# The first DeltaNet step of each layer: roundings, masks, one block load and the places of the level products

## What is computed

```python
SEQ, D_MODEL, DEPTH = 1024, 1024, 2
DN_HEADS, DN_DK, DN_DV, DN_CHUNK = 8, 128, 128, 64
qkv = silu(causal_conv(concat([dq, dk, dv]), conv_w))
...
def gated_deltanet(q, k, v, beta, g):
    gc = cumsum(g)                                   # inside a chunk
    decay = exp(where(causal, gc[:, None] - gc[None, :], -inf))
    L = where(strict, (k * beta) @ k.T * decay, 0)   # strictly lower triangle
    sol = triangular_solve(L + eye, concat([v * beta, k * beta * exp(gc)]))
    u, w = split(sol)
    attn = (q @ k.T) * decay
    # then over the chunks, in order:
    v_new = u - w @ state
    o = (q * exp(gc)) @ state + attn @ v_new
    state = state * exp(gc_last) + (k * exp(gc_last - gc)).T @ v_new
```

## Time and profile before

| | |
|---|---|
| median of 3 runs | 2674.55 us |
| the profiled execution's own time | 2673.82 us |
| its span, first to last instruction | 2672.0 us |
| TensorE busy | 2637.4 us (99%) |
| VectorE busy | 1728.2 us (65%) |
| ScalarE busy | 679.5 us (25%) |
| GpSimd busy | 827.1 us (31%) |
| DMA engines, mean busy share of slices | 1 to 5 tenths |

### The profile page before, as it was taken

The page is one execution under the profiler, slowest core; times in us unless marked ns, Lnnn a source line. Parts: engine busy times, 40 slices in busy tenths (PEclk is TensorE's granted clock), DMA queues, the critical chain, the costliest instruction groups (busy, mean ns, idle before and its releaser), DMA issues.

```text
span 2672.0 us, 39928 instructions
## 1 busy us (share of the span) xinstructions
PE 2637.4 (99%) x14850; PEld 2254.4 (84%) x14850; DVE 1728.2 (65%) x3856; ACT 679.5 (25%) x1367; POOL 827.1 (31%) x455
## 2 busy tenths in 40 slices
PE   7999999999999999999999999999999999999998
PEld 5788888888888899888878888888888998888886
DVE  7878777877756555434587778777877555653333
ACT  5333333232312222200142332323232211230001
POOL 3233323333312122435422333332323122133443
PEclk9999999999999999999999999999999999999999
DMA  4322222222211112434532222222222111133344
GB/s 171 96 79 62 74 75 75 66 73 76 71 52 44 42 34 72 128 95 123 163 93 84 76 72 65 74 78 70 67 71 77 43 50 42 40 109 99 95 142 142
DMA packets 292836, 217.83 MB, mean 82 GB/s; under 512 B 31682, under 2 KB 246036, under 8 KB 292388
## 3 DMA queue, kind: packets, MB, share of 16 engines
q1 hardware_dynamic: 254322, 151.21, 19.7%
q10 hardware_dynamic: 38322, 64.07, 7.0%
HBM read 176.37 MB, written 38.86 MB: 81 GB/s over the span
## 4 chain that ended last, share of the span: by engine, by line
PE 91%; DVE 4%; DMA 2%; issue 1%; ACT 1%; POOL 1%; SPq 1%; ACTq 0%; DVEq 0%; POOLq 0%
PE dense_ps L773 22%; PE dense_ps L777 22%; PE dense_ps L775 22%; PE work L756 3%; PE dense_ps L797 2%; PE dense_ps L798 2%; PE dense_ps L799 2%; PE work L1028 1%; PE work L1065 1%; PE work L1085 1%; PE work L1004 1%; PE work L987 1%; PE work L1054 1%; PE work L1078 1%; PE work L1039 1%
## 5 line engine op out<-in xcount | busy, mean ns | idle before, releaser
L773 PE MATMUL dense_ps<-act_hi,w_hi 128*128 128x512 f32 x2560 | 1051.9, 411 | 2.4 <-POOL act_lo L2382 2.2
L777 PE MATMUL dense_ps<-act_hi,w_lo 128*128 128x512 f32 x2560 | 1002.3, 392 | 0.0
L775 PE MATMUL dense_ps<-act_lo,w_hi 128*128 128x512 f32 x2560 | 1000.3, 391 | 0.0
L2361 POOL TENSOR_TENSOR w_lo<-w_raw,w_hi 128x1024 fp32r<-128x1024 f32 x162 | 399.7, 2467 | 1013.8 <-ACT w_hi L1299 570.6
L777 PEld LDWEIGHTS dense_ps<-act_hi,w_lo 128*128 128x128 f32 x2560 | 480.7, 188 | 106.9
L773 PEld LDWEIGHTS dense_ps<-act_hi,w_hi 128*128 128x128 f32 x2560 | 482.7, 189 | 85.6 <-issue 3.2
L775 PEld LDWEIGHTS dense_ps<-act_lo,w_hi 128*128 128x128 f32 x2560 | 483.2, 189 | 79.7 <-issue 0.5
L1797 DVE SCALAR_TENSOR_TENSOR arena<-arena,cols 128x512 f32<-128x512 f32 x288 | 242.2, 841 | 5.1
L1299 ACT ACTIVATE w_hi<-w_raw 128x1024 fp32r<-128x1024 f32 x88 | 92.7, 1054 | 327.8 <-PE dense_ps L777 155.4
L1289 ACT ACTIVATE arena<-dense_ps 128x512 f32<-128x512 f32 x96 | 57.4, 598 | 264.0 <-PE dense_ps L777 264.0
L756 PE MATMUL work<-mk,arena 128*128 128x128 f32 x768 | 111.8, 275 | 9.8 <-issue 7.5
(11 more groups left out here) (239 smaller groups left out, 4034.2 us busy)
## 6 DMA issues: line engine op xcount, KB each, us to landing
w_raw<-in_w_in SPq DMA_DIRECT2D x138, 512.0 KB, 3.8
gate_scratch<-arena ACTq DMA_DIRECT2D x64, 256.0 KB, 2.5
arena<-gate_scratch ACTq DMA_DIRECT2D x64, 256.0 KB, 2.7
arena<-l_scratch SPq DMA_DIRECT2D x62, 256.0 KB
w_raw<-in_w_out SPq DMA_DIRECT2D x18, 512.0 KB, 3.8
o_scratch<-arena ACTq DMA_DIRECT2D x32, 256.0 KB, 2.0
w_raw<-in_w_up_dn SPq DMA_DIRECT2D x16, 512.0 KB, 3.7
arena<-o_scratch ACTq DMA_DIRECT2D x32, 256.0 KB, 3.8
```

Source lines behind the costliest of these rows:

```text
L773: eng.matmul(dense_ps[:, to, :], w_hi[:, slot, k, :], hi[:, k, seg], start=(k == 0), stop=False)
L775: eng.matmul(dense_ps[:, to, :], w_hi[:, slot, k, :], lo[:, k, seg], start=False, stop=False)
L777: mm = eng.matmul(dense_ps[:, to, :], w_lo[:, slot, k, :], hi[:, k, seg], start=False, stop=(k == KT - 1))
L2361: eng.tensor_tensor(w_lo[:, slot, :, :], w_from[second][:, :, :], w_hi[:, slot, :, :].bitcast(F32), ALU.subtract)\
```

## The change

It touches the first unit of each layer, and the block load of all units.

- Roundings: of the four weight blocks that the first unit prepares, `split` 1 to 3 are made by ScalarE (`split_hi`); the low parts stay on VectorE and become a step of their own, `low`. `split` 0 stays on VectorE.
- Masks: in the first unit `mask` runs on VectorE instead of GpSimd; for half 1 the second mask is a step of its own, `mask_t`.
- Block load: one transfer of 512 KB on SyncE's queue in every unit. In the first unit ScalarE's queue issues no part of it, and its load of the next weight block (GR0) and of `gcb` for half 1 move to the step `kq` and wait until the blocks have landed.
- Order: `solve` starts at slot 16 instead of 17, `spread` stands at 21 instead of 24; `level_v` stands at slots 23, 26 and 29 and `level_x` at 25, 28 and 31 (before: 25, 28, 31 and 27, 30, 33). `kq` on TensorE moves from slot 16 to 17, and its VectorE part becomes the step `kq_decay` at 25. `qe` moves from 15 to 23. The convolution of v is dealt out differently: its last steps stand at the unit's end, three of them ahead of `vt`.

```diff
-        at(6, "mask", 0)
-        at(8, "dec", 0)
+        at(8, "split", 1)
+        at(9, "mask", 0)
+        at(9, "dec", 0)
         at(10, "nl", 0)
+        at(10, "low", 1)
...
-        at(15, "qe")
-        at(16, "kq")
-        slots[15].insert(0, ("mask", 1))
-        at(19, "dec", 1)
-        solve, spread_at, vt = 17, 24, 34
+        at(17, "kq")
+        at(20, "split", 2)
+        at(21, "spread")
+        at(21, "turn", 0)
+        at(22, "low", 2)
+        at(23, "level_v", 0)
+        at(23, "mask", 1)
+        at(23, "qe")
+        at(25, "level_x", 0)
+        at(25, "kq_decay")
+        at(25, "mask_t", 1)
+        at(26, "turn", 1)
+        at(26, "level_v", 1)
+        at(26, "dec", 1)
+        at(26, "split", 3)
+        at(28, "level_x", 1)
+        at(29, "turn", 2)
+        at(29, "level_v", 2)
+        at(29, "low", 3)
+        at(31, "level_x", 2)
+        solve, spread_at, vt = 16, 21, 34
...
-            spread(0 if solve <= n < spread_at else 1 if n < solve else 2)
+            spread(1 if n < solve or n in (22, 23, 29, 30, 31) else 2 if n > 31 else 0)
...
-        def l_source(c):
+        def l_source():
 
-            return l_dram[:, c:c + 2, :, :].rearrange("a c i k -> a (c i k)").unsqueeze(1)\
-                .to_broadcast([NB, BASE, 2 * BASE * BASE])
+            return l_dram[:, :, :, :].rearrange("a c i k -> a (c i k)").unsqueeze(1)\
+                .to_broadcast([NB, BASE, CPH * BASE * BASE])
...
-                    for c in range(0, CPH if u else 2, 2):
-                        eng.dma_start(lb[:, c:c + 2, :], l_source(c)).then_inc(l_in.sem, 16)
+                    eng.dma_start(lb[:, :, :], l_source()).then_inc(l_in.sem, 16)
...
-                        elif what == "split" and kind in ("even", "odd"):
+                        elif what == "split" and (kind in ("even", "odd") or kind == "first" and step[1]):
...
-                            eng.dma_start(gcb, row_dram[0:1, HALF:SEQ].to_broadcast([P, HALF])).then_inc(row_in.sem, 16)
...
-                            if kind == "first":
-                                eng.wait_ge(l_st.sem, l_st.after(tn, 16 * NB))
-                                eng.wait_ge(sv_s.sem, sv_s.after(tn, 0))
-                                eng.dma_start(lb[:, 2:CPH, :], l_source(2)).then_inc(l_in.sem, 16)
...
-                            if kind == "first":
-                                eng.wait_ge(w_lo_ok.sem, w_lo_ok.after(n + BLK_FIRST + 3, 0))
-                                eng.dma_start(w_raw[:, :, :], w_src(l, w_in, GR0)).then_inc(w_in_ok.sem, 16)
+                        elif what == "kq" and kind == "first":
+                            eng.wait_ge(l_in.sem, l_in.after(tn, 16))
+                            eng.wait_ge(w_lo_ok.sem, w_lo_ok.after(n + BLK_FIRST + 3, 0))
+                            eng.dma_start(w_raw[:, :, :], w_src(l, w_in, GR0)).then_inc(w_in_ok.sem, 16)
+                            eng.dma_start(gcb, row_dram[0:1, HALF:SEQ].to_broadcast([P, HALF])).then_inc(row_in.sem, 16)
...
+                        elif what == "mask" and kind == "first":
+                            w = tn + step[1]
+                            eng.wait_ge(row_in.sem, row_in.after(w, 16))
+                            eng.tensor_tensor(decl[(nb + step[1]) % 2], bcast4(mk[:, C_NL:C_NL + P]), chunk_rows,
+                                              ALU.subtract).then_inc(m_ok.sem, 1)
...
-                        elif what == "kq":
+                        elif what == ("kq_decay" if kind == "first" else "kq"):
```

More of the change, by code:

```diff
@@ L179, in unit_schedule @@
             at(solve + k // 3, "solve", k)
-        at(spread_at, "spread")
-        for n in range(NLV):
-            if first or n:
+        for n in range(NLV if not first else 0):
+            if n == 0:
+                at(spread_at, "spread")
+            if n:
                 at(spread_at + 1 + 3 * n, "turn", n)
@@ L224, in unit_schedule @@
                 break
-            if pieces % (2 * KT) == 0 and (pieces or kind not in ("first", "odd_last")):
+            if pieces % (2 * KT) == 0 and not first and (pieces or kind != "odd_last"):
                 step = ("split", pieces // (2 * KT))
[L227 to L230, removed]
+                waiting.insert(0, step)
                 if kind == "even_last" and step[1] == 2:
@@ L510, in build @@
         nl_ok, sv_s = signal("neg_l_ready", 1), signal("solve_steps", 2 * BASE - 2)
-        l_st, l_in = signal("l_blocks_stored", 16 * NB), signal("l_blocks_loaded", 32)
+        l_st, l_in = signal("l_blocks_stored", 16 * NB), signal("l_blocks_loaded", 16)
         xs_ok = signal("solve_start_ready", 1)
@@ L1914, in delta_unit @@
                     ns_of = slice(CPH * nb, CPH * nb + CPH)
+                    chunk_rows = gcb.rearrange("p (c t) -> p c t", c=CPH)
                     for step in unit_schedule(kind):
@@ L1936, in delta_unit @@
                                 split_v(l, 0, idx - BLK_RET - 2)
-                            elif kind not in ("even", "odd"):
+                            elif kind not in ("even", "odd", "first"):
                                 eng.wait_ge(w_hi_ok.sem, w_hi_ok.after(g + idx, 0))
                                 split_w(g + idx, idx % 2)
-                            if kind == "first":
+                            elif kind == "first" and step[1] == 0:
+                                split_w(g + idx, idx % 2)
                                 low_w(g + idx, idx % 2)
+                        elif what == "low":
+                            idx = g0 + step[1] + 1
+                            low_w(g + idx, idx % 2)
+                        elif what == "mask" and kind == "first":
[3 more added lines that the diff above has]
+                                              ALU.subtract).then_inc(m_ok.sem, 1)
+                            if step[1] == 0:
+                                eng.tensor_tensor(dect, chunk_rows, bcast4(mk[:, C_NT:C_NT + P]), ALU.add)\
+                                   .then_inc(m_ok.sem, 1)
+                        elif what == "mask_t":
+                            w = tn + step[1]
+                            eng.wait_ge(row_in.sem, row_in.after(w, 16))
+                            eng.wait_ge(aT_ok.sem, aT_ok.after(w, 0))
+                            eng.tensor_tensor(dect, chunk_rows, bcast4(mk[:, C_NT:C_NT + P]), ALU.add)\
+                               .then_inc(m_ok.sem, 1)
                         elif what == "evac" and kind == "odd_last":
@@ L2074, in delta_unit @@
                                 eng.wait_ge(xs_ok.sem, xs_ok.after(tn, 1))
-                                eng.wait_ge(l_in.sem, l_in.after(tn, 32))
+                                eng.wait_ge(l_in.sem, l_in.after(tn, 16))
                             else:
@@ L2433, in delta_unit @@
                                 split_w(g + idx, idx % 2)
-                        elif what == "mask":
+                        elif what == "mask" and kind != "first":
                             w = tn + step[1]
```

## The result

The changed kernel takes 2680.07 us as the median of 20 executions (2671.94 to 2684.52), the one before 2674.56 us (20 executions, 2672.53 to 2676.39): a ratio of 1.0015 with a 95% interval of 1.0009 to 1.0021. By the ratio it is slower by about 4 us (by the medians 5.5), where 6.5 us less were forecast, and the time lies outside the range. The spread is part of the result: before, the executions lie within 4 us; now they lie within 12.6, and 14 of 20 are above 2678 us.

What follows compares the result with a forecast made beforehand. TensorE, busy 99% of the span, was taken to bound the kernel, so gains come from its waits. From 2674.55 us, 5.3 (first units) and 1.2 (other units) were subtracted, giving 2668.1 us; range 2665.0 to 2672.0.

Steps and rivals of the forecast that it cites:

- signs of being wrong: Solve starts after 74.5, a level product waits over half a microsecond, or block load holds VectorE in over five units.
- the block load's landing: First unit: block load issued at 68.6 lands at 73.8, the solve starts there, block diagonal done at 81.5.
- the other units: Later units: block load lands 0 to 1 us sooner, 0.4 in each of three waiting units, 1.2 us in all.
- the nothing at which it put the order of the transfers at the unit's end: End of first unit: no cost counted for transfer order; `l_scratch` stores called unchanged, table load counted only as ScalarE time.
- The masks: First unit: a mask on VectorE takes 0.69 us, so `nl` runs at 64.0, 1.2 us earlier.
- the lone row: Profile row of a block load with nothing beside it: 5.1 us from issue at 147.89 to data passed.
- The late end of the prediction, 75.7: Latest landing allowed for the first unit's block load; the bound for both first units is then 2 x 1.3 us.
- The other levels: First unit, level products behind the first: no wait counted, the least certain zero, 0.3 us spare at the third level.
- Given back: First unit's `xu` waits 0.8 us for `vt`, shrinking 3.6 to 2.8; layer 0 loses another 0.3 on ScalarE.
- the 5.3 of the prediction: Gain of both layers' first units together: 2.5 + 2.8 us, from TensorE waits removed less what is given back.
- Rival C: Block load: one transfer is no faster, one issue fewer saves nothing; 2669.3 us, chance 0.17.
- E: Later units: the single transfer lands some 2 us later, 15 units pay 0.9 us each; 2682.8 us, chance 0.06.

## Why the prediction was wrong

All three of its signs of being wrong came: the solve starts at 75.39, the first level waits 0.75 and 1.15 us, and the block load holds VectorE in 15 units. Three of its steps failed: the block load's landing, the other units, and the nothing at which it put the order of the transfers at the unit's end.

**The masks**: right. 0.69 us on VectorE, `nl` at 64.22 against 64.0, the block load's issue at 68.83 against 68.6. The masks' place is only a part of it: from the mask's start to `nl` it is 3.23 us before, 2.18 in the change and 2.79 with the masks back on GpSimd, so 0.6 us come from the place and 0.4 from the new order, which has no convolution step beside the mask. What was not priced is the second mask: on GpSimd it cost the solve 1.0 us.

**The block load's landing**: wrong, and the first failing step: "so I take the lone row: it lands at 73.8". That row was of two transfers, and ended with the last packet. Here the packets moved from 70.3 to 74.4 us, with two parts from 70.2 to 74.1, and the solve started 1.0 us behind the last packet with one transfer, 0.5 behind it with two. So of the 1.6 us by which it was late about 1.0 is the time behind the last packet, which the row did not have. In the first units of all traces that have the new order, the packets take 4.0 to 4.6 us from first to last with one transfer (12 cases) and 3.4 to 4.2 with two (12 cases), and issue to solve is 6.6 to 7.4 us with one and 5.6 to 6.4 with two. The late end of the prediction, 75.7, was nearer, but was given for other loads ahead of the blocks. TensorE came to the first level at 82.45, as worked out (82.2); the block diagonal came 1.6 us late, so there was a wait of 0.75.

**The other levels**: right. The zeros that were called least certain held: in the change no level product behind the first waits.

**Given back**: right. A wait at `xu` of 0.67 and 0.68 against 0.8. That layer 0 loses 0.3 more on ScalarE was wrong: the table's load took 0.34 us to issue there, not 1.34.

With the load in two parts and the table out of the way, the first units give 4.7 us: in the second trace of that version TensorE is 2.2 us ahead of the kernel before behind the first of them, and 2.7 ahead of and 5.2 behind the second. That is nearly the 5.3 of the prediction.

**Other units**: wrong in sign. "I let the load land 0 to 1 us sooner, 0.4 as the value" was +1.2 us of gain; one load alone costs 3.5 us (2677.58 against 2674.10), a part of which its trace shows. Rival C, that one load is no faster, was nearer, and E had the direction (later in several units that have little to spare), with four times the size. C's rule on the number of engines (the Trainium skill, "DMA: Bandwidth & Descriptors", section "Why a DMA increments its semaphore by 16 and not by 1") was not tried: one form and the other have it alike. The traces agree with it: alone, the block load's packets took 48.0% of the time of 16 engines (70.3 to 74.4 us in the change), the table's 83.3%.

**What was not in the sum at all**: the order of two queues at the unit's end. The prediction follows the table's load as time on ScalarE, and says that the `l_scratch` stores are unchanged; it set the time behind it at nothing, and did not set the new issue times of that load and of DZ0 against the stores and the block load of the second unit. Before, `xu` of the second layer started at 1421.83, with the block load 3.8 us and the table's load 1.1 us ahead of it. In the change `xu` comes earlier, against it the stores stand 2 us later, and DZ0's load is issued with the last of them. When all goes well the block load is still 3.8 us ahead of `xu` and the table's 0.6 (1415.62 and 1418.79 against 1419.41). When a store is held, it falls behind DZ0, the block load leaves 0.2 us ahead of `xu` (1421.92 against 1422.14) and behind the table, and the execution loses some 5 us. Three of the four traced executions of the change have it. This fits the medians, 2673 with the table moved against 2676 and 2680 without, but these are not all of one chip, and how many of the executions without a trace have it is not known.

## What to carry to other kernels

When a stage is made earlier, list the transfers at its end on all queues in order of issue, before and after: a big transfer that nobody waits for yet, issued some tenths of a microsecond ahead of a small one that bounds the next stage, can hold it for most of its own duration (here about 3 us, with 3.4 us for the big one). Such a load belongs where the queue is empty, not at a stage's border. And price a merged transfer from rows of a merged one, from issue to the instruction that waits, not to the last packet.

## What the runs showed of the hardware that was not expected

- One transfer of 512 KB (4 KB rows) released its waiter 1.0 to 1.3 us behind its last recorded packet in the first units; two of 256 KB (2 KB rows) on the same queue 0.4 to 0.9 us. Why is open.
- Of two transfers issued on two queues 0.39 us apart, the first moved nearly all of its 1 MB before the second moved anything: the queues did not share. In the trace with two parts the table's load moved first although its issue began 0.09 us behind that of the blocks (1416.33 against 1416.24).
- A short VectorE operation with two inputs beside a GpSimd mask took 1.15 us instead of 0.19, and ended with the mask. The Trainium skill, "SBUF — State Buffer", section "SBUF: two separate sides", says that such an operation and a GpSimd one that reads this memory lock one port pair for a whole instruction, and that the later one waits; the rows agree.
- Half clock came behind some of TensorE's waits and not behind others. Each of the four of 2.7 to 3.5 us had a stretch of 3.4 to 6.8 us at 0.5 beside or behind it. Of those of 1.5 to 1.9 us, the one in the earlier trace rows and its like in the second layer, and the ones with one load alone, had none; the one of 1.61 with the masks on GpSimd and one of 1.57 with the table's load first had 3.4 us; with `vt` first, the 1.94 of the first layer had none and the 1.92 of the second had 3.4. Near 1360 us, at the border of the layers, 3.4 us of it stand in most traces of all kernels, and not in all.
